# The second layer's projections of a two-layer trunk as seven half-size products each, with attention paced by them

## The reference

```python
def diff_mixer(h, w_in, lam_q, lam_k, subln_g, w_out, rel_bias, layer_idx):
    q, k, v, z = jnp.split(h @ w_in, [BRANCH, 2 * BRANCH, 3 * BRANCH], axis=-1)   # each 2048 wide
    # q, k: 8 heads x 2 maps x 128; v, z: 8 heads x 256
    for each block of 128 queries:
        s = q . k * scale + bias[t5_bucket(distance)], causal      # two maps m
        p = softmax(s)
        a = p[:, :, 0] - lam * p[:, :, 1]
        o = a @ v                                                   # 256 wide
    o = o * rsqrt(mean(o*o) + eps) * subln_g * (1 - lambda_init)
    return (o * silu(z)) @ w_out
```

## Time and profile before

| | |
|---|---|
| median of 3 runs | 2772.97 us (2769.8 to 3203.12) |
| profiled execution, slowest core | span 2768.0 us |
| spans of the eight cores | 2754.6 to 2768.0 us |
| the profiled execution's span under the median | 5.0 us |
| TensorE, VectorE, ScalarE, GpSimd busy | 2629.6, 1369.3, 1240.4, 214.4 us |
| instructions | 60261 |

### The profile page before, as it was taken

One profiled execution on the slowest core, in us unless ns is written; L12 is line 12 of the kernel. 1 busy time (PEld: TensorE's weight loads), 2 busy tenths in 40 slices (PEclk: granted clock), 3 DMA queues, 4 the chain that ended last, 5 costly groups with the idle time before them and its releaser, 6 DMA issues.

```text
span 2768.0 us, 60261 instructions; the slowest of 8 cores (2754.6 to 2768.0 us)
## 1 busy us (share of the span) xinstructions
PE 2629.6 (95%) x19886; PEld 1589.9 (57%) x20130; DVE 1369.3 (49%) x3834; ACT 1240.4 (45%) x3256; POOL 214.4 (8%) x412
## 2 busy tenths in 40 slices
PE   6799999999999998999999999999999999998998
PEld 4477777777777785444445544454545554543443
DVE  2544444444444443565423635455555455555666
ACT  0365555555555563343214443444444444533431
POOL 2000000000000000000000110111011111110110
PEclk9999999999999999999999999999999999999999
DMA  9222222223222239999814242534334344487653
GB/s 156 43 47 42 40 41 40 41 42 50 45 40 41 41 55 196 216 240 235 184 31 81 56 76 51 81 63 74 70 71 70 66 71 83 103 153 163 182 163 131
DMA packets 355728, 254.31 MB, mean 92 GB/s; under 512 B 280800, under 2 KB 298080, under 8 KB 350816
## 3 DMA queue, kind: packets, MB, share of 16 engines
q1 hardware_dynamic: 311184, 158.00, 24.3%
q0 software_dynamic: 44240, 92.44, 20.8%
HBM read 224.21 MB, written 58.26 MB: 102 GB/s over the span
## 4 chain that ended last, share of the span: by engine, by line
PE 84%; DMA 5%; DVE 3%; SPq 3%; issue 3%; ACT 1%; another core or an unknown queue 1%; DVEq 0%; POOL 0%; ACTq 0%; POOLq 0%
PE pb L336 42%; PE pb L511 13%; PE pb L498 13%; PE pb L655 4%; PE pb L640 4%; PE pb L1061 4%; PE pb L972 4%; DMA M<-M 2%; SPq L1210 1%; DMA x1b<-M 1%; DMA A<-xs 1%; DVE M L1043 1%; SPq L808 1%; ACT M L1014 1%
## 5 line engine op out<-in xcount | busy, mean ns | idle before, releaser
L643 ACT ACTIVATE M<-pb,M 128x256 bf16<-128x256 f32 (+1 forms) x1152 | 521.3, 461 | 408.5 <-PE pb L655 341.2
L336 PE MATMUL pb<-M,B 128*128 128x512 bf16 (+1 forms) x2122 | 526.2, 374 | 6.3 <-DVE M L916 3.7
L336 PE MATMUL pb<-B,M 128*128 128x512 bf16 x2058 | 517.5, 380 | 7.2 <-DMA B<-xs 3.8
L1014 ACT ACTIVATE M<-pb 128x512 bf16<-128x512 f32 (+3 forms) x512 | 264.6, 523 | 276.8 <-PE pb L972 249.1
L336 PEld LDWEIGHTS pb<-B,M 128*128 128x128 bf16 x2112 | 206.1, 98 | 204.4 <-issue 7.5
L655 PE MATMUL pb<-M 128*128 128x129 bf16 x2176 | 311.7, 221 | 1.8 <-DVE M L647 0.4
L640 PE MATMUL pb<-M 128*128 128x256 bf16 (+1 forms) x1152 | 307.0, 267 | 6.1 <-ACT M L643 4.6
L336 PEld LDWEIGHTS pb<-M,B 128*128 128x128 bf16 x2176 | 212.2, 98 | 174.7 <-issue 5.9
L655 PEld LDWEIGHTS pb<-M 128*128 128x128 bf16 x2176 | 206.5, 98 | 81.4 <-issue 5.4
L336 PE MATMUL pb<-B,A 128*128 128x512 bf16 x1002 | 236.2, 383 | 6.3 <-DMA B<-w1o 4.1
L511 PE MATMUL pb<-M,A 128*128 128x128 bf16 x3360 | 236.2, 219 | 0.1
(11 more groups left out here) (110 smaller groups left out, 2670.0 us busy)
## 6 DMA issues: line engine op xcount, KB each, us to landing
M<-w0s POOLq DMA_DIRECT2D x30, 1024.0 KB, 11.0
M<-x SPq DMA_DIRECT2D x16, 1024.0 KB, 6.2
x1d<-M SPq DMA_DIRECT2D x32, 512.0 KB, 5.2
M<-w1qk POOLq DMA_DIRECT2D x16, 1024.0 KB, 9.2
M<-w1vz POOLq DMA_DIRECT2D x8, 2048.0 KB, 17.2
M<-x1d SPq DMA_DIRECT2D x16, 1024.0 KB, 5.5
y<-M SPq DMA_DIRECT2D x32, 512.0 KB, 3.2
A<-w0o POOLq DMA_DIRECT2D x4, 2048.0 KB, 39.2
```

What stands on the lines that cost most here:

```text
L336: ins = e.matmul(out, lhsT=lhs(kc), rhs=rhs(kc), start=(kc == 0), stop=(kc == KC - 1))
L643: P.op("act", lambda e: e.activation(out=pt.ap[:, 0:w], in_=pb[s][:, 0:w], func=AF.Exp, bias=bs.ap[:, j * 8 + I:j * 8 + I + 1], scale=SCAL ...
L1014: P.op("act", lambda e: e.activation(out=self.p.ap[:, lo:lo + nb * 128], in_=pb[s][:, 0:nb * 128], func=AF.Exp, scale=SCALE, accum_out=st. ...
```

## The change

The second layer's projections are computed as heads 1 to 15 of the first layer are: seven products for each projection of a head (its 256 columns as two halves of 128) and each half of the tokens. `unit(u, kind, p)` is one such piece: head u, kind k, q, v or z, token half p. q and k keep 512 columns, v and z go to 128. x1 stays in `B` with its sums in `A` (`xq`); of 11 slots of 2 KB (`wfree`), four take raw weights and three their sums for each projection (`load_w1`, `sum_w1`). k has two buffers, q, v and z one. Attention items carry positions within the stream of units (`DiffT.add`), `pump` issues them when the stream gets there, and barriers (`bar_q`, `bar_pv`, `bar_fin`) issue what is left before a buffer is overwritten. p and its transpose share one space of 17,408 bytes; PV has two banks, projections three.

In the first layer the sums of x for the second token half and of w move into the work beside them. In the first epilogue `x1b` goes: `x1_tr` transposes from SBUF. The first step of both epilogues takes three blocks and then one, with column parts in another order; a half of one part of w0o is loaded a head earlier. In the last head g comes by transposes on TensorE (`tr`, `h7`) for all 16 blocks, where it was for three pairs. Products, sums and transposes are otherwise what they were; the result is the same function.

```diff
-        xbf = V("M", oW + 16384, 4096)
+        xbf = [V("M", oW + 16384, 4096), V("M", oW + 20480, 4096)]
...
+        xq = [[V("B", p * 32768 + i * 8192, 8192) for i in range(4)] + [V("A", p * 24576 + i * 8192, 8192) for i in range(3)] for p in range(2)]
...
+        def wino7(W, X, fm, tm, fin):
...
             def done(k, b):
...
                 elif k == 2:
+                    fin(11, b, None)
+                elif k == 5:
+                    fin(22, b, U)
+                elif k == 4:
+                    fin(21, b, T)
+                else:
+                    fin(12, b, T)
...
         def x1_tr(b):
             tc, lo = b // 4, (b % 4) * 128
+            xb = xbf[b % 2]
             d = big["B"][:, tc * 8192:(tc + 1) * 8192].rearrange("p (c t) -> p c t", c=KC)[:, :, lo:lo + 128]
-            P.dma("sp", "xt", lambda e: e.dma_start_transpose(out=d, in_=x1b[b * 128:(b + 1) * 128, :]),
-                  reads=[("x1b", b, b + 1)], writes=rx("B", tc, 0, KC, lo, lo + 128))
+            P.dma("sp", "xt%d" % (b % 2), lambda e: e.dma_start_transpose(out=d, in_=xb.ap),
+                  reads=xb.r, writes=rx("B", tc, 0, KC, lo, lo + 128))
...
+        def sum_w1(n, extra=None):
...
+            for o, a, b in ((4, 1, 0), (1, 3, 1), (5, 3, 4), (6, 2, 5)):
+                sub_v(w[o], w[a], w[b], 0, ALU.subtract)
...
+        def unit(u, kind, p):
...
+                def stt():
+                    P.op("dve", lambda e: e.scalar_tensor_tensor(out=H.ap, in0=H.ap, scalar=1.0, in1=src, op0=ALU.add, op1=ALU.mult),
+                         reads=rsrc + H.r, writes=H.r)
+                    P.op("dve", lambda e: e.tensor_tensor(out=z3[:, st * 4:st * 4 + 4, m * 128:(m + 1) * 128], in0=b4(H.ap),
+                                                          in1=gain.ap[:, m * 128:(m + 1) * 128].unsqueeze(1).to_broadcast([128, 4, 128]), op=ALU.mult),
+                         reads=H.r + gain.r, writes=zbuf.rr(st * 1024, st * 1024 + 1024))
...
+                if kind < 2:
+                    d = qbuf if kind else kbuf[u % 2]
+                    lo = m * 2048 + st * 512
+                    put(d.ap[:, lo:lo + 512], d.rr(lo, lo + 512), b, add)
+                elif kind == 2:
+                    put(v3[:, st * 4:st * 4 + 4, m * 128:(m + 1) * 128], vbuf.rr(st * 1024, st * 1024 + 1024), b, add, b4)
+                elif add is None:
+                    gate(pb[b][:, :], bank(b), st, m)()
+                else:
+                    tsum(tm.Z, add, b)
+                    sc.after(1200, gate(tm.Z.ap, tm.Z.r, st, m))
+            return wino7(wun[4 * u + kind], xq[p], kind < 2, tm, fin)
...
-        rP, rA = Ring(oPP, PPN), Ring(oAT, ATN)
+        ring = Space(oX, RING)
...
             def comb(self):
...
-                P.op("dve", lambda e: e.scalar_tensor_tensor(out=c(16), in0=s0, scalar=256.0 * RMS_EPS, in1=s0, op0=ALU.mult, op1=ALU.mult),
-                     reads=rs, writes=rc(16))
+                P.op("pool", lambda e: e.tensor_tensor(out=c(16), in0=s0, in1=s0, op=ALU.mult), reads=r0, writes=rc(16))
...
+                self.t = V("M", self.p.off + 2 * w, 2 * w)
...
+            def pump(self, pos):
+                if self.can_q() and self.qk[0][4] <= pos:
+                    self.do_q()
+                self.start()
+                if self.pv and self.pv[0][2] <= pos:
+                    sc.run(self.pv.popleft()[:2])
...
+        def flow(F):
+
+            for it in F:
+                DT.pump(fpos["t"])
+                sc.run(it)
+                fpos["t"] += it[0]
...
-        for f in sum_x(1):
-            f()
-        sum_w0(0)
...
+                    if u == 1 and i == 0:
+                        for k in range(0, 16, 2):
+                            G.insert(2 + 2 * k, call(s1[k]))
+                            G.insert(3 + 2 * k, call(s1[k + 1]))
...
+            if n == 7:
+                for k, f in enumerate([f for k, f in enumerate(sums0) if k % 4 < 2]):
+                    G.insert(16 + 5 * k, call(f))
+                for k, f in enumerate([f for k, f in enumerate(sums0) if k % 4 >= 2]):
+                    G.insert(len(G) if k > 4 else 64 + 5 * k, call(f))
...
+        seq = [(0, k, 0) for k in range(3)] + [(0, k, 1) for k in range(3)] + [(0, 3, 1), (0, 3, 0)]
         for u in range(1, ND):
+            for k in range(4):
+                ps = (0, 1) if u == ND - 1 or (u == ND - 2 and k == 3) else (1, 0)
+                seq += [(u, k, p) for p in ps]
...
+            if u and k == 1:
+                flow([call(bar_q, u - 1, p)])
+            if u and k == 2:
+                flow([call(bar_pv, u - 1, p)])
+            if u and k == 3:
+                flow([call(bar_fin, u - 1, p)])
+            if k == 2 and second and u < ND - 1 or (u, k, p) == (ND - 1, 2, 0):
                 if u < ND - 1:
+                    order = P1 + P0 if u < ND - 2 else P0 + P1
+                    DT.add(u, order, at[n], at[n + 6] - 2000, at[n + 1] + 4000, at[n + 7] + 4000)
+                else:
+                    DT.add(u, range(8), at[n], at[n + 2], at[n + 1] + 5000, end - 4000)
+                    DT.add(u, range(8, 16), at[n + 2], end + 45000, end, end + 65000)
+            G = unit(u, k, p)
...
+        load_wo(1, 2)
+        load_gp(1, 0, 14)
+        load_wo(1, 3)
```

More of the change, by code:

```diff
@@ L1177, in tr @@
                 P.op("pe", f, reads=g.r + ident.r, writes=bank(s))
[L1178 to L1190 removed]
+                t = h7[I]
@@ new lines, in build_program, with bar_q, bar_pv, bar_fin @@
+        DT = DiffT()
+        fpos = {"t": 0.0}
+        def flow(F):
[3 more added lines that the diff above has]
+                fpos["t"] += it[0]
+        def bar_q(u, p):
+            left = lambda: not any(x[2].u == u and x[2].i // 8 == p for x in DT.qk)
+            DT.until(left)
+        def bar_pv(u, p):
+            DT.until(lambda: all((u, i) in done_pv for i in range(16) if p == 0 or i >= 8))
+        def bar_fin(u, p):
+            DT.until(lambda: all((u, i) in done_fin for i in range(p * 8, p * 8 + 8)))
```

775 lines of the change are left out of this document (391 added, 384 removed).

## The result

The changed kernel takes 2816.59 us (median of 4 runs, 2812.25 to 2836.14), the kernel before beside it 2781.15. The ratio is 1.0158, with a 95% interval from 1.0102 to 1.0213: 1.6% slower. Forecast were 2670 us and a range of 2615 to 2760. The profiled execution (core 1) has a span of 2810.7 us, 42.7 over the one of before.

A forecast was written before the change was run, and what follows sets the result against it. TensorE, busy for 95% of the span, was taken as the bound, its waits and slow clock counted too. Sum: 2768.0 - 97.4 - 14 - 21 + 28 + 1 = 2664.6, plus 5.0 from span to median: 2670 us, range 2615 to 2760.

The forecast's parts named there:

- GpSimd: GpSimd's queue: one small product more and 128 weight loads for 24, between -2 and +10 us, charged at nothing.
- shrink: Second layer's z halves: VectorE's waits, above all for transposes to release p (50.8 us), shrink as VectorE falls behind.
- The clock: Second layer's z halves: TensorE runs partly at 1.2 GHz after a wait, 2.3 us lost on the mean.
- VectorE in the z halves: Second layer's 16 halves of z: VectorE about even with TensorE, costing 0 to 78 us, taken as 28.
- The start: Before the first layer's head 1: the wait for sums of x and w goes, -14 us, between -8 and -15.5.
- The first epilogue: First layer's end: waits for w0o and transposed g go, less +6 for new work: -21 us, between -27 and 0.
- The second epilogue: Kernel's last stage: +1 us for g's transposes on TensorE, otherwise left as it is, +-12 us.
- The seven products: Second layer's projections: seven products for eight save 12.2 us a head, 97.4 us over eight heads, on TensorE.
- a band to which I gave 0.03: The outcome of few barrier hits with the time within 2%, 0.03 of the barriers rival's 0.12.
- The weights: Rival: 128-column matmuls wait for their weight loads, 42 ns each, 302 us: 2970 us; chance 0.02.
- Waits are not removed: Rival: products only are shortened and the waits stay, 2704 us, within the forecast's range; no chance of its own.
- The barriers are hit: Rival, second layer's heads: blocks unfinished at 42 barriers run without products, about 12.2 us each; 16 hits 2865 us; chance 0.12.

The follow-up runs named there:

- noload: Changed kernel with the second layer's weight loads from its second head on replaced by GpSimd writing zeros: 2748.36 us, ratio 0.988 to the kernel before.
- spread: Changed kernel with weight loads moved from bursts to one behind every second product of the next projection's first half: 2771.84 us, ratio 0.9986 to the kernel before.
- c_pace: s_poolgain with the order counting a PV bank free after 2,500 ns (was 1,000) and the near scores' buffer 1,000 ns later: 2739.39 us, ratio 0.9871.
- c_all: s_poolgain with the edits of c_z, c_pace and c_tail together: 2722.93 us, ratio 0.9817 to the kernel before.
- `start`: Kernel before with only the start's sums (x's second half, w) moved into head 0's last and head 1's first products: 2767.79 us, ratio 0.9961.
- c_z: s_poolgain with a second place for z's sum and the gate 2,400 ns behind it in the order (was 1,200): 2754.9 us, ratio 0.9922.
- x_nogate: c_all with z as tanh alone, written by ScalarE, without VectorE's gate product and GpSimd's gain: ratio 0.9805 to the kernel before.
- x_both: c_all without the second layer's weight loads from the fourth projection on and without gate and gain: ratio 0.9781 to the kernel before.
- nogain: Changed kernel without VectorE's multiplication of z by the per-head gain (64 operations): 2802.49 us, ratio 1.0088 to the kernel before.
- s_poolgain: spread with z's product with the gain on GpSimd instead of VectorE: 2759.72 us, ratio 0.9911 to the kernel before.
- x_noload: c_all with the second layer's weight loads from the fourth projection on replaced by GpSimd writing zeros: ratio 0.9809 to the kernel before.
- c_tail: s_poolgain with w1o in pieces, g of blocks 2 and 3 loaded earlier, the last eight blocks' PV 14 us later: 2765.15 us, ratio 0.9952.
- s_tail: spread with w1o loaded in smaller pieces and g of blocks 2 and 3 loaded 15 us earlier: 2764.66 and 2768.65 us, no ratio.

## Why the prediction was wrong

**The step that failed** is *GpSimd*, "between -2 and +10 us, and I charge nothing". It priced the time of issue of 128 loads, not what the loads do to the DMA transposes on which PV waits. Measured: without the loads 0.028 of the time, 77 us (noload), and 69 us of the heads; by spacing them 0.017, 48 us (spread), and 54 us of the heads. So the bursts are the greater part of what the loads cost, and the heads were 119 us over the forecast by the same medians. The profile of before held the warning: VectorE's 50.8 us were slow transposes. I read them as a matter of VectorE's queue, and added that the waits "shrink". They did not: beside the loads slow transposes are twice as frequent as before (24% over 6 us for 12%, 1% without the loads), and PV stands closer behind the subtraction. The constant in the order isn't what brought it closer: its least distance was 8,000 ns before and is 8,500 now. The tighter space and the barriers are the likely reason, and no run shows it.

**PV banks and the near scores' buffer.** The second step is a term that isn't in the sum at all. L1115 waits 29.3 us for L1161 in after, and c_pace, which lets the order reuse both 1,000 to 1,500 ns later, takes 34 us off the heads. Its waits for PV banks fell by 14 of them (22 to 8.5) and those for transposes too, from 20 to 28 us by core to some 10. In the time of the whole kernel it is only some 11 us, as 19 come back in the last stage.

**The clock.** In the sum for the second layer's heads I priced slow clock behind waits, at 2.3 us each, only for z. In the heads of after the granted clock is 0.95 for 1083 us, some 50 us, partly within matmuls that are counted as busy. In c_all it is 0.99. How much of each experiment's gain is wait and how much clock isn't separated here; the two go together in every run.

**VectorE in the z halves.** I took 28 us between 0 and 78 (4.9 a half), and the size was about right. In spread z's two halves took 17.5 and 20.1 us (their 224 products, mean of heads 1 to 5) where TensorE was busy for 16.1 and 17.3: 4.2 a head, some 29 in seven heads. The gain on GpSimd took 13 us off the heads and the second place for z's sum 14. What was wrong is the way to it: the sum, tanh, gate, gain is a serial chain, and the mean load (675.8 us over seven heads, 96.5 a head, for the 90.7 of the forecast) told nothing of it; VectorE waited 71.5 us for tanh in after (32 times, 1500 to 2434 us).

**The start.** -14 was within 1 us for the stage, and wrong as a gain: the next stage is 12.9 us longer, with L662 (3.9 us) and L510 (3.3) waiting for VectorE, and L709 for 5.1 more: these are the transposes of the first layer's last head, now on TensorE, which `start` doesn't contain. On the median core the first epilogue begins 2.1 us earlier than before; `start` has 5.9. I had named "11 us of VectorE ahead of the evacuations, beside some 7 of TensorE", and still set the bound at -8.

**The first epilogue.** -14.9 for -21: the waits for w0o and g are gone, as said; new are 5.1 us in three waits behind L773 and 3.3 before the second layer's first product.

**The second epilogue,** left "+-12 us": 5.3 us longer in after. It has one wait of 22.7 us for a transpose that took 30.3 us beside w1o, where the kernel before had 8.8 us in three waits for transposes and 4.1 for w1o:

```profile
2533.10 30.33 DMA M<-M
```

Four edits give part of what they take off the heads back here: c_z 7 us, c_pace 19, x_nogate 10 and x_both 14. Noload, nogain, spread, s_poolgain and x_noload don't. The longest single wait for a transpose isn't the whole reason. By core it is 21 to 31 us in after, 20 to 39 in spread, 19 to 52 in c_z, 27 to 32 in x_both, but 11 to 19 in c_pace and 9 to 11 in c_all, whose last stages are long all the same. c_all gave 0.009 over s_poolgain where c_z alone gave nothing; of the 40 us that it takes off the heads 34 are there in c_pace alone.

**What held.** The seven products: 224 matmuls of 128 columns and a little attention in c_all's v halves take 14.0 and 14.8 us with TensorE busy throughout, so the price of 55.8 ns stands, and with it the 97.4 us. By the 81 ns of the Trainium skill (TensorE: Matmul & The Clock Gate, Back-to-back issue gap) those 224 alone would be 18.1 us, an estimate from the page's figure; the trace does not agree. TensorE's work a head came to 129.4 to 129.8 us for the 127.7 forecast.

**The rivals.** The time fell in a band to which I gave 0.03. The weights fell as a cause. "Waits are not removed" was nearly right of the start, where all but about 2 us of the removed wait came back, and explains nothing of the second layer's heads. *The barriers are hit* had the right sign and the right symptom, TensorE before PV in gaps of 5 us and more, and the wrong cause: by the order only 33 entries in the whole second layer are run without products between, and leaving out the loads removes 48 of 49.5 us of these waits with every barrier in place. A sign that two mechanisms share decides nothing. The rivals that were missing: loads in bursts slow the transposes, and the order hands out a PV bank or a buffer before it is free.

**The ledger of c_all** against the forecast, by its profile: start and first layer's heads +15.3 us, first epilogue +11.5, the second layer's heads +13.3, last stage +16.0, in all 56.1. **Open:** how the last stage's DMA, w1o and g against p's transposes, could be relieved (cutting it up shortened the stage by 5 us in c_tail and 21 in s_tail, and no time of the whole kernel shows it), which part of c_pace's edit does its work, and what the last 2.8 us a head are.

## What to carry to other kernels

When transfers are made smaller and issued as slots come free, ask which latency-critical DMA runs beside them, and price its slowest case rather than its median. Look in the profile for who waited for that DMA before: a wait on an engine with slack becomes the pace when the distance between producer and consumer shrinks. Release loads one by one at set places in the order, and let the order count a bank as free by the length of the chain that frees it: when fewer banks are left, keep at least the distance that the old order had. Read each experiment by stage as well as by its ratio, since a later stage can take back what an earlier one gained.

## What the runs showed of the hardware

- A DMA transpose of one block's p took 3.2 us at the median, 6.1 at most without weight loads (6.3 over all eight cores), 12.2 beside four 256 KB loads, 30.3 and 37.3 beside loads of 2 MB. The issuing instruction on SP can stand with it (32.94 us for one of p, 18.43 for one of g), and held what was queued behind.
- At a wait of 7.3 us TensorE's granted clock was 0.50 over 6 us, from 1646 to 1652 us, the last 3 of the wait and the 3 behind it; in a head of c_all whose longest wait was 1.6 us it was 1.00 in every window.
- GpSimd multiplied 128x512 f32 by f32 into bf16 in 1265 ns where VectorE took 692; moved there it still paid (s_poolgain, 13 us of the heads), on an engine that was 11% busy in after.
